# Two chained model blocks: four small tiles grow, and most tiles behind them start 32 to 96 bytes later

## What is computed

```python
p = split_proj(h @ w_in[l])                     # first block: L786, L1021 and others
y = (g[:, :, 0] * (ret @ w_br_ret[l]) + g[:, :, 1] * (dsa @ w_br_dsa[l])
     + g[:, :, 2] * (gl @ w_br_gla[l]))
y = y @ w_out[l]                                # first block: L1114
q, k, v, u, vv, gate = jnp.split(hl @ w_in, EVEN_SPLITS, axis=-1)           # L1179, L1132
y = (jnp.concatenate([a, b], axis=-1) * jax.nn.silu(gate)) @ w_out          # L1132
```

## The kernel before, in words

| line | where | stationary high, low | moving high, low |
|---|---|---|---|
| L786 | first block, projections (`project_split`) | xhi1, xlo1 | whi1, wlo1 |
| L1021 | first block, merge gates (`merge_half`) | xhi1, xlo1 | merge_high, ring_low |
| L1114 | first block, output projection | y_high, xlo1 | out_high, ring_low |
| L1179 | even layer, q, u and v in pieces | xhi, xlo | whi, ring_low |
| L1132 | even layer, gates and output (`project_wide`) | xhi, xlo | wide (the last quarter: wide_late), ring_low |

## Time and profile before

### The profile page before, as it was taken

One profiled execution on the slowest core, in us unless ns is written; L12 is line 12 of the kernel. 1 busy time (PEld: TensorE's weight loads), 2 busy tenths in 40 slices (PEclk: granted clock), 3 DMA queues, 4 the chain that ended last, 5 costly groups with the idle time before them and its releaser, 6 DMA issues.

```text
span 1077.4 us, 13519 instructions
## 1 busy us (share of the span) xinstructions
PE 1042.0 (97%) x5208; PEld 757.8 (70%) x5208; DVE 601.1 (56%) x1177; ACT 477.9 (44%) x942; POOL 76.6 (7%) x103
## 2 busy tenths in 40 slices
PE   7999999999999999999999999999999999999997
PEld 5688875777467888857874587777677888556553
DVE  2429966595655299754454744236745555245742
ACT  3437547462134365476540353246535423225641
POOL 3001110000000020110000000500000001230000
PEclk9999999999999999999999999999999999999999
DMA  9645432476624355335467362422642015242000
GB/s 385 277 164 203 182 134 101 156 293 276 251 90 170 140 208 203 113 130 219 189 243 304 121 234 79 156 98 79 235 157 103 1 40 220 112 156 98 2 1 39
DMA packets 13743, 171.29 MB, mean 159 GB/s; under 512 B 1504, under 2 KB 1760, under 8 KB 3056
## 3 DMA queue, kind: packets, MB, share of 16 engines
q1 hardware_dynamic: 13216, 168.82, 41.0%
q10 hardware_dynamic: 464, 1.61, 0.4%
HBM read 169.37 MB, written 1.05 MB: 158 GB/s over the span
## 4 chain that ended last, share of the span: by engine, by line
PE 83%; DVE 7%; ACT 6%; DMA 2%; issue 1%; SPq 0%; DVEq 0%; ACTq 0%
PE bank L786 15%; PE bank L1132 8%; PE bank L1081 8%; PE bank L1021 7%; PE bank L1179 6%; PE bank L756 5%; PE bank L1138 5%; PE bank L1114 4%; PE bank L1316 3%; PE bank L764 3%; PE bank L866 3%; PE bank L1393 2%; PE bank L719 2%; PE bank L1381 1%; PE bank L727 1%
## 5 line engine op out<-in xcount | busy, mean ns | idle before, releaser
L1505 ACT ACTIVATE whi<-ring 128x512 fp32r<-128x512 f32 x120 | 73.6, 631 | 65.3 <-PE bank L786 65.3
L2169 DVE TENSOR_TENSOR wlo<-ring,whi 128x512 fp32r<-128x512 f32 x120 | 82.2, 708 | 32.8 <-ACT whi L1505 32.5
L786 PE MATMUL bank<-whi,xhi 128*128 128x512 f32 (+1 forms) x256 | 98.2, 384 | 1.3 <-ACT dsag L1428 1.3
L786 PE MATMUL bank<-wlo,xhi 128*128 128x512 f32 (+1 forms) x256 | 96.4, 377 | 0.0
L786 PE MATMUL bank<-whi,xlo 128*128 128x512 f32 (+1 forms) x256 | 96.4, 376 | 0.0
L764 PE MATMUL bank<-ring,hT 128*128 128x512 f32 (+1 forms) x160 | 61.2, 536 | 0.2 <-ACT hT L1448 0.2
L1138 PE MATMUL bank<-ring,hT 128*128 128x256 f32 (+2 forms) x224 | 57.9, 418 | 3.3 <-ACT hT L1471 2.3
L1021 PE MATMUL bank<-merge_high,xhi 128*128 128x512 f32 x144 | 58.2, 404 | 1.6 <-ACT retqkv L1428 1.1
L1021 PE MATMUL bank<-ring_low,xhi 128*128 128x512 f32 x144 | 56.9, 395 | 0.0
L1021 PE MATMUL bank<-merge_high,xlo 128*128 128x512 f32 x144 | 56.9, 395 | 0.0
L786 PEld LDWEIGHTS bank<-whi,xhi 128*128 128x128 f32 x256 | 48.2, 188 | 11.8 <-ACT dsag L1428 1.6
(11 more groups left out here) (414 smaller groups left out, 2198.3 us busy)
## 6 DMA issues: line engine op xcount, KB each, us to landing
ring<-in_weights SPq DMA_DIRECT2D x73, 2048.0 KB, 8.1
ring<-in_weights SPq DMA_DIRECT2D x5, 1024.0 KB, 5.0
ring<-in_weights SPq DMA_DIRECT2D x2, 1360.0 KB, 10.3
ring<-in_weights SPq DMA_DIRECT2D x1, 1536.0 KB, 8.3
kk<-in_k SPq DMA_DIRECT2D x1, 1120.0 KB, 7.7
X<-in_x SPq DMA_DIRECT2D x1, 1024.0 KB, 14.6
kc<-in_k ACTq DMA_DIRECT2D x1, 1024.0 KB, 10.6
X<-in_context SPq DMA_DIRECT2D x1, 1024.0 KB, 10.1
```

The costliest lines, as they stand in the source:

```text
L786: mm = pe.matmul(o[:, 0:width], a, b[:, q % BUFFERS, at], start=(k == 0 and m == 0), stop=(k == KD - 1 and m == 2))
L1505: act.activation(whi1[:, q % BUFFERS, :], w, ACT.Copy).then_inc(event("hi1_ready"), 1)
L2169: dve.tensor_tensor(wlo1[:, q % BUFFERS, :], piece1(q)[2], whi1[:, q % BUFFERS, :], ALU.subtract).then_inc(event("lo1_ready"), 1)
```

## The change

Four tiles are opened larger, and the places that used them whole now name the part that is used. What is computed, and every instruction's size, stays.

```diff
-        pw = sb("pw", [P, 2])
+        pw = sb("pw", [P, 16])
...
-        idx = sb1("idx", [P, TT, 324])
+        idx = sb1("idx", [P, TT, 328])
...
-        posf = sb1("posf", [P, TT])
+        posf = sb1("posf", [P, 16])
...
-        nsink = sb2("nsink", [P, 8])
+        nsink = sb2("nsink", [P, 16])
...
-                    copy_out(u, f"idx{t}", idx[:, t, :])
+                    copy_out(u, f"idx{t}", idx[:, t, 0:324])
...
-            step(pool.tensor_copy(posf[:], posi))
+            step(pool.tensor_copy(posf[:, 0:TT], posi))
...
-            step(dve.tensor_scalar(nsink[:], sink, -1.0, None, ALU.mult))
+            step(dve.tensor_scalar(nsink[:, 0:8], sink, -1.0, None, ALU.mult))
```

## The result

| | time, us |
|---|---|
| before, 22 runs | 1078.26 (1076.87 to 1080.33) |
| the change, 22 runs | 1081.52 (1078.69 to 1083.80) |
| ratio, with its 95% interval | 1.0021 (1.0012 to 1.0030) |
| forecast | 1073.7 (1072.5 to 1077.9) |

The change is slower by 0.2%, where 0.35% faster was forecast. The span of its profiled execution is 1081.5 us. Runs of either kernel have short stretches, different from run to run, in which TensorE's clock is granted at the lower level, and the times of one kernel spread over 3 to 5 us. The two medians, 0.30% apart, therefore say less than the ratio with its interval.

A forecast was written before the change was run, and what follows sets the result against it. PE, busy 97% of the span, was taken as the bound. Gains of 1.01 (L1114), 1.56 (L1179) and 1.87 us (L1132), 4.44 less settling and a wait, left 3.75: 1077.4 to about 1073.7 us, range 1072.5 to 1077.9.

The forecast's parts named there:

- rows 3 to 6: Profile rows of PE matmul starts: aligned L786 at 226.6 ns, shifted L1114, L1179, L1132 at 232.1 to 232.6.
- The last row group: Rows 6, last block of L1132: moving wide_late and ring_low aligned, only stationary xhi not; 0.2332 us a matmul.
- the moving one hardly counts: From L1132's last block at 0.2332 us: the stationary operand's start matters, the moving operand's hardly.
- the 5.5 ns: Claimed excess of each shifted matmul over the aligned 226.6 ns, used to price L1114 and L1179.
- the 283 distances of L1179: Matmul-to-matmul distances in L1179's five blocks, priced at 5.5 ns each: 1.56 us to gain.
- the settling: Aligned blocks also start slower; 0.03 us for each of 21 blocks, 0.63 us, taken off the 4.44 us sum.
- the forecast's own range: Range for the whole kernel if the main forecast holds, without the rivals: 1072.8 to 1074.8 us.
- The grain is 128 bytes: Rival: float32r operands the change puts at 64 are as bad as at 96; 1078.4 to 1081.2 us; chance 0.18.
- the case in which the moving tile counts too: 128-byte grain with moving operands at 64 also slow: L786 and L1021 rise to 232.1 ns; +3.8, 1081.2 us.
- No gain: Rival: something else, such as tile pairs read at once, slows L1114, L1179, L1132 and stays; 1077.4 us; chance 0.13.
- Swallowed: Rival: PE arrives 4 us earlier but waits for DVE, ACT or a weight load; about 1075.8 us; chance 0.04.
- The rule of the Trainium skill that was weighed: SBUF's grain is 16-byte lines, so starts at multiples of 32 are already aligned; change worth 0 us instead of 3.75.

The follow-up runs named there:

- e_all64: e_128 with a pad ahead of ring_low moving every tile 64 bytes on, so every float32r operand starts at 64 modulo 128; 1080.26 us, ratio 1.0027 to before.
- e_256_all32: e_256 with a pad moving every tile 32 bytes on, so all float32r operands start at 160 modulo 256; 1075.56 us, ratio 0.9978 to before.
- e_256_mov: e_256 with only moving tiles (merge_high, whi1, wlo1, wide) moved by 64 bytes; 1078.87 us in one run, before 1078.96.
- e_256: The change with idx and nsink enlarged so all float32r operands start at 128 modulo 256; 1074.37 us, ratio 0.9953 to before; again 1075.60, 0.9964.
- e_128: The change with idx and nsink enlarged so all float32r operands start at 0 modulo 128; 1080.76 us, ratio 1.0025 to before.
- the second measurement: The change, unaltered, run again beside before on the same chip; 1079.83 us in 11 runs, ratio 1.0021 to before.
- e_256_low: e_256 with only low stationary tiles moved, xlo1 by 64 bytes and xlo by 128; 1079.52 us in one run, before 1078.96.

## Why the prediction was wrong, point by point

**The step that failed** is the reading of rows 3 to 6: that three lines lag because an operand of theirs starts at 32 modulo 64. The comparison had two things that differed together. L786 and L1021 of before have all four tiles at 128 modulo 256 (58496, 144256, 152448, 160640 and 1152 all leave 128). L1114, L1179 and L1132 have theirs at 96 and 128. I saw "32 off a multiple of 64", and it was "32 off each other". e_all64 and e_256_all32 part the two: moving everything by 64 or by 32 changes no rate at 512 columns, and e_256_all32 has 226.7 ns with every start at 32 modulo 64.

**What the change then did.** Modulo 256, the four edits together bring y_high, xhi, whi and wide from 96 to 128, and out_high from 96 to 192. They also take xlo1, xlo, whi1, wlo1, merge_high and wide_late from 128 to 192. So L1114, L1179 and L1132 traded a distance of 32 for one of 64, worth about 1 ns at L1179 and L1132 and nothing that lasts at L1114, and L786 and L1021, where nothing had been wrong, got a distance of 64 too.

**Where the table misled.** It gave starts by 64 and by 128. By 128, all tiles of L786 and L1021 read 0 and those of the other three 96 and 0, which fits both readings. I took the absolute one and never listed "alike with each other" as a rival. The last row group, L1132 with wide_late at 233.2 ns, was the place to doubt: with its moving tile at a multiple of 64 it is slower than with wide at 96. I read it as "the moving one hardly counts"; e_256_mov shows one moving tile off by 64 at 233.3 ns.

**A reading that was wrong without harm.** The prediction took the clock to be in full in every slice. A 9 in that row is 90% or more: before has its clock at the lower level for some 3.4 us at 28 us and again at 239 us, as the windows above show. Both lie outside the rows that the 5.5 ns come from. And the 283 distances of L1179 count the first start of each block, which the terms of the two other lines leave out; that is 0.03 us.

**The size was right.** The forecast was 3.75 us for bringing L1114, L1179 and L1132 to the pace of the others: e_256, which does that, has -3.7 us by lines (the dips apart), made up of 0.92 at L1114 (forecast 1.01 before the settling was taken off), 1.27 at L1179 (1.56) and 1.55 at L1132 (1.87). Nothing was swallowed behind. Its first median, 1074.37 us, is within the forecast's own range of 1072.8 to 1074.8; the second, 1075.60, is above it.

**The rivals.** "The grain is 128 bytes" had the sign and, for the case in which the moving tile counts too, L786 and L1021 rising and L1114 hardly moving, as it went. Its mechanism fell all the same: by it e_128 should have been faster than before, and it was as slow as the change. Its bracket, 1078.4 to 1081.2, holds the 1079.83 of the second measurement and not the 1081.52 of the first; where it holds, that is luck, since its cause was not the right one. "No gain" named the cause in passing, which pairs of tiles are read at once, and had the time wrong: it took for granted that the new offsets leave the pairs as they were. "Swallowed" didn't happen. The rule of the Trainium skill that was weighed (page "SBUF — State Buffer", section "Specifications (TRN2)", lines of 16 bytes) gives 0 us for the change, and the lines show +2.3; it says nothing of two tiles' starts against each other.

**The chances.** 0.65 lay on one reading of a comparison that the trace could not part from another. The outcome, 0.21% slower (0.12 to 0.30%), lies on the line between "slower", which was given 0.09, and "same", which was given 0.26.

## What to carry to other kernels

For float32r matmuls with 512 moving columns, compare the starts of the tiles that are read together, modulo 256, and give the pads that make them alike; a multiple of 64 for each by itself is neither needed nor enough. e_256 does this with the same four tiles, a few hundred bytes larger, and beats before by 0.4% (0.9953 and 0.9964) and with it the change. For 256 moving columns the advice doesn't hold, as e_256_mov shows, and other widths were not tried. And where a trace seems to hold a comparison ready, write the addresses with more than one modulus and look for a second difference between the two sides before pricing the first; a variant that moves everything by the same amount is the cheapest test of it.

## What the runs showed of the hardware

- The pace of a stream of float32r matmuls, 128 stationary and 512 moving columns, is 226.7 ns with all starts alike modulo 256 and 228.9 to 234.3 otherwise. The same pattern of starts gives the same pace, to about 1 ns, whichever line and tiles it is: 128, 192, 128, 128 gives 231.1 at L1179 in the change and at L786, L1021 and L1114 in e_256_low. Some patterns waver: 128, 192, 192, 128 is at 231.1 in some blocks and at 232.2 in others of the same line. Distances that are whole multiples of 256 cost nothing: in before, xhi1 and xlo1 are 85760 apart, 335 times 256, and L786 holds 226.7.
- With 256 moving columns the order turns: 120.0 ns with all starts alike, 113.3 to 118.9 otherwise. Why is open.
- By groups of three, at 512 columns, it is 680 ns, and 686.7, 693.3, 696.7, 700 or 703 where starts differ. Most of these are whole steps of 6.7 ns, so the time lost looks like a few fixed pieces in each group. That this is the reading of the stationary and of the moving tile meeting in the memory is my guess; no run shows it.
- Plain float32 matmuls with 256 moving columns didn't notice: a stretch of 64 fills 13.81 us at L866 and at L1316 before and after, though hT moved by 64 bytes and hT2 by 32. (The 64 are the profile's records; the loops issue 32 matmuls there, two records for each.)
- 226.7 ns is also more than one cycle for each of the 512 columns, which at the 2.4 GHz level would be 213 ns. The Trainium skill, page "TensorE: Matmul & The Clock Gate", section "Back-to-back issue gap", gives about 216 for a single gap and about 131 for a sustained stream of pairs at 512 columns. No stream of float32r with 512 columns went below 226.7 here. What makes the difference stays open.
- The short dips of the granted clock are part of a run's spread: the 22 runs of the change reach from 1078.69 (mean clock 0.998) to 1083.80 (0.993). They are not all of it, since runs of before at one mean clock, 0.994, lie over 4 us apart. Rates from the timeline show in one profile what the medians of a few runs hardly do.
